# The token mixer of a hybrid decoder layer: chunk by chunk over all heads after the in-projection, or head pair by head pair between its last tiles

## What is computed

```python
x = x + 0.5 * post1(ffn1(pre1(x)))
P = pre_m(x) @ w_in        # 2816 columns: q 512 | k 128 | v 128 | hq 512 | hf 512 | hi 512 | hg 512
A = sliding-window attention(q, k, v)     # 8 query heads, 2 key heads, window 128, rotary, sinks
# HGRN2, 8 heads of 64: f = lb + (1-lb)*sigmoid(hf); k = 1-f; G = cumsum(log f)
#   S_new = exp(G_end) * S + (k*exp(G_end-G))^T hi ;  o = (hq*exp(G)) @ S + intra-chunk part
H = rms_norm(o) * silu(hg)
x = x + post_m(concat(A, H) @ w_out)
x = x + 0.5 * post2(ffn2(pre2(x)))
```

## Time and profile before

| what | value |
|---|---|
| median of three runs | 2332.66 us (2326.21 to 2344.02) |
| span of the profiled execution | 2344.2 us |
| its own time beside the span | not given apart; the highest of the three runs is 2344.02 us |
| in-projection, steady part 832 to 1062 us | TensorE busy 229.02 of 230, granted clock 1.00 |
| mixer, 1062 to 1390 us | TensorE busy 267.73 of 328, granted clock 0.73 |
| VectorE busy in the same 328 us | 230.07 |
| sample stage, 1390 to 1432 us | TensorE clock 0.54 |

### The profile page before, as it was taken

The page is one execution under the profiler, slowest core; times in us unless marked ns, Lnnn a source line. Parts: engine busy times, 40 slices in busy tenths (PEclk is TensorE's granted clock), DMA queues, the critical chain, the costliest instruction groups (busy, mean ns, idle before and its releaser), DMA issues.

```text
span 2344.2 us, 34327 instructions
## 1 busy us (share of the span) xinstructions
PE 2203.1 (94%) x13257; PEld 2071.8 (88%) x13257; DVE 1158.7 (49%) x1871; ACT 581.9 (25%) x852; POOL 428.6 (18%) x256
## 2 busy tenths in 40 slices
PE   6999999999999899997787887979999999999996
PEld 5999999999999799995555557969999999999996
DVE  3445444444544732226777665264444454444446
ACT  5111111111111631013343324162111111111113
POOL 6110010111110231103343311041111011110100
PEclk9999999999999999996777667989999999999998
DMA  3111111111111111110000001201111111111111
GB/s 120 55 46 45 54 45 40 49 45 45 45 54 46 75 63 54 45 45 19 0 0 0 31 31 52 108 18 55 46 45 54 36 45 54 45 45 54 45 36 72
DMA packets 28174, 108.83 MB, mean 46 GB/s; under 512 B 4178, under 2 KB 4826, under 8 KB 26337
## 3 DMA queue, kind: packets, MB, share of 16 engines
q1 hardware_dynamic: 28128, 108.20, 13.6%
HBM read 97.37 MB, written 10.81 MB: 46 GB/s over the span
## 4 chain that ended last, share of the span: by engine, by line
PE 84%; DVE 8%; ACT 3%; issue 3%; POOL 1%; DMA 0%; DVEq 0%; SPq 0%; ACTq 0%; POOLq 0%
PE PS L329 26%; PE PS L330 25%; PE PS L331 25%; DVE resid L1102 2%; PE PS L497 2%; PE PS L499 2%; PE PS L468 1%; PE PS L515 1%; DVE y L1097 1%; PE PS L365 1%; DVE dif L1296 1%; DVE q_dec L1307 1%; DVE mx L1358 1%; ACT sm L952 1%; DVE sm L1353 0%
## 5 line engine op out<-in xcount | busy, mean ns | idle before, releaser
L329 PE MATMUL PS<-x_hi,w_hi 128*128 128x344 f32 x2832 | 913.4, 323 | 49.5 <-DVE w_lo L1084 24.1
L330 PE MATMUL PS<-x_lo,w_hi 128*128 128x344 f32 x2832 | 908.1, 321 | 0.0
L331 PE MATMUL PS<-x_hi,w_lo 128*128 128x344 f32 x2832 | 906.7, 320 | 0.0
L329 PEld LDWEIGHTS PS<-x_hi,w_hi 128*128 128x128 f32 x2832 | 536.1, 189 | 54.3 <-issue 22.7
L330 PEld LDWEIGHTS PS<-x_lo,w_hi 128*128 128x128 f32 x2832 | 536.2, 189 | 0.9
L331 PEld LDWEIGHTS PS<-x_hi,w_lo 128*128 128x128 f32 x2832 | 536.1, 189 | 0.0
L624 POOL TENSOR_TENSOR raw<-raw,vecs 128x1024 f32<-128x1024 f32 x110 | 212.2, 1931 | 1439.1 <-DMA raw<-in_w_gu 1243.5
L1192 DVE TENSOR_TENSOR y<-y,PS 128x344 f32<-128x344 f32 x528 | 264.8, 511 | 182.9 <-PE PS L331 182.7
L329 PE MATMUL PS<-h,w_hi 128*128 128x344 f32 x1056 | 339.6, 322 | 0.7 <-DVE h L1156 0.3
L330 PE MATMUL PS<-h,w_hi 128*128 128x344 f32 x1056 | 337.6, 320 | 0.0
L331 PE MATMUL PS<-h,w_lo 128*128 128x344 f32 x1056 | 336.6, 319 | 0.0
(11 more groups left out here) (188 smaller groups left out, 1613.5 us busy)
## 6 DMA issues: line engine op xcount, KB each, us to landing
raw<-in_w_gu SPq DMA_DIRECT2D x88, 512.0 KB, 3.3
raw<-in_w_down SPq DMA_DIRECT2D x44, 512.0 KB, 3.3
raw<-in_w_in SPq DMA_DIRECT2D x22, 512.0 KB, 3.3
resid<-in_x SPq DMA_DIRECT2D x3, 1376.0 KB, 9.2
stream_x<-resid SPq DMA_DIRECT2D x3, 1376.0 KB, 4.7
resid<-stream_x SPq DMA_DIRECT2D x3, 1376.0 KB, 10.2
out_y<-resid SPq DMA_DIRECT2D x3, 1376.0 KB, 4.7
raw<-in_w_out SPq DMA_DIRECT2D x8, 512.0 KB, 3.3
```

The source lines that it names most:

```text
L329: nc.tensor.matmul(PS[:, bank, :GW], wh, vh, start=(k == 0), stop=False)
L330: nc.tensor.matmul(PS[:, bank, :GW], wh, vl, start=False, stop=False)
L331: mm = nc.tensor.matmul(PS[:, bank, :GW], wl, vh, start=False, stop=(k == last))
```

## The change

The in-projection's tiles get another order: k, v, q (4 tiles), then for each head pair hf, hq, hi, then hg. Nine tiles (`EARLY`) run as a stage of their own. Beside them keys and queries are rotated over all tokens (five times three matmuls of 344 columns, `rotate(r)`, and VectorE's `rope(r)`), and the values are transposed once for all chunks.

The other 13 tiles (39 units) are spread over eight bodies written out one after the other, five units a body, each cut into two halves of 12 matmuls that stand in the `gap`s of TensorE's order. Body i does one head pair (i // 2) for four chunks of HGRN, and all attention heads for chunk i. Gates are made per head pair: `gates(t+1)` on VectorE and `logs(t+1)` on ScalarE in the odd bodies, `sigmoid(t+1)` at the end of the even ones. The state becomes block diagonal (`Sbd`, 128 x 128 for a head pair), so that the part of the output that comes from the state is four full products; the four chunks' states are made one from the other on VectorE (`states()`), before TensorE may compute `outputs()`. The masked copies of a level become one instruction where they were two. The silu of hg moves behind the mixer. The samples' three loads are issued when the last body's attention has been copied, since their memory is in use till then. In the diff the orders of `body(i)` stand one after another: TensorE's (from `level(0)`), ScalarE's (from the second `level(1)`), VectorE's (from `def states()` with `seq`).

```diff
+T_K, T_V, T_Q, T_F, T_G = 0, 1, 2, 6, 18
+EARLY = 9
+BODIES, BODY_UNITS = 8, 5
...
-            sp.wait_ge(S["scan_done"], 4 * N_CH)
+            sp.wait_ge(S["attc_done"], N_CH)
+            sp.wait_ge(S["a_done"], 5 * BODIES)
             sp.dma_start(state_s[:], ins["state"]).then_inc(S["smp_in"], 16)
             sp.dma_start(k_win_s[:, :, 0:WINDOW - 1], ins["k_cache"]).then_inc(S["smp_in"], 16)
             sp.dma_start(v_win_s[0:WINDOW - 1], ins["v_cache"]).then_inc(S["smp_in"], 16)
...
+                def gap(x):
+                    if x // 2 < len(units) and units[x // 2] is not None:
+                        half_unit(units[x // 2], x % 2)
...
+                def outputs():
+                    pe.wait_ge(S["st_done"], i + 1)
+                    pe.wait_ge(S["k_done"], 7 * i + 2)
+                    pe.wait_ge(S["a_done"], 5 * i + 5)
+                    for j in range(TPH):
+                        nc.tensor.matmul(PS[:, 7, j * CH:(j + 1) * CH], Sbd[:, j, :], qg[:, j, :], start=(j == 0), stop=False,
+                                         skip_group_check=True)
+                    for hd in range(N_HEADS):
+                        j, r = hd // 2, slice(HEAD * (hd % 2), HEAD * (hd % 2 + 1))
+                        mm = nc.tensor.matmul(PS[r, 7, j * CH:(j + 1) * CH], V[:, TPH * b + j, r], A[:, hd, :],
+                                              start=False, stop=(hd >= N_HEADS - 2), skip_group_check=True)
+                    mm.then_inc(S["o_done"], 1)
...
                 level(0)
+                gap(0)
+                if b == 0:
+                    values()
+                gap(1)
                 level(1)
                 scores(0)
+                gap(2)
                 level(2)
+                gap(3)
                 level(3)
+                gap(4)
                 scores(1)
                 level(4)
+                gap(5)
+                keys_by_token()
+                gap(6)
                 probs_by_key(0)
+                gap(7)
+                states()
+                attend(0)
+                gap(8)
                 probs_by_key(1)
+                outputs()
+                gap(9)
+                attend(1)
...
                 level(1)
+                unit_end(0)
                 level(2)
+                if b == 1 and t < TPH - 1:
+                    logs(t + 1)
+                unit_end(1)
                 level(3)
                 level(4)
                 exponentials(0)
+                unit_end(2)
...
                 probs(0)
+                unit_end(3)
+                if i < BODIES - 1:
+                    first_decays(i + 1)
...
+                if b == 0 and t < TPH - 1:
+                    sigmoid(t + 1)
+                unit_end(4)
...
+                def states():
+                    if i:
+                        dve.wait_ge(S["o_done"], i)
...
+                    for j in range(TPH):
+                        for o in range(2):
+                            r = slice(HEAD * o, HEAD * (o + 1))
+                            dst = state[r, t, :] if b and j == TPH - 1 else Sbd[r, j + 1, r]
+                            up = nc.vector.scalar_tensor_tensor(dst, Sbd[r, j, r], g_end[r, j:j + 1], PS[r, 2, j * HEAD:(j + 1) * HEAD],
+                                                                ALU.mult, ALU.add)
+                        if j < TPH - 1:
+                            seq(up)
...
+                level(i, 2)
+                q_decayed(i, 1)
+                weights(0)
+                q_decayed(i, 2)
+                unit_end(0)
+                if b and t < TPH - 1:
+                    gates(t + 1)
+                level(i, 3)
+                weights(1)
+                q_decayed(i, 3)
                 sub_max(0)
+                unit_end(1)
+                level(i, 4)
                 weights(2)
+                q_decayed(i, 4)
                 weights(3)
                 over(0)
                 sub_max(1)
+                unit_end(2)
                 weights(4)
+                if i + 1 < BODIES:
+                    start(i + 1)
+                unit_end(3)
                 over(1)
+                if i + 1 < BODIES:
+                    q_decayed(i + 1, 0)
+                states()
+                unit_end(4)
```

More of the change, by code:

```diff
@@ L64, in __call__, with tile_of, body_units @@
         ins.then_inc(self.sem, 1)
[L65 to L73, removed]
+        self.eng.wait_ge(self.sem, self.n)
+def tile_of(v):
+    n = EARLY + v // NG
+    return n, v % NG, v % 2, n % 2
+def body_units(i):
+    first = BODY_UNITS * i
+    if i < BODIES - 1:
+        return [first + j for j in range(BODY_UNITS)]
+    return [None] + [v for v in range(first, N_LATE)]
 def build(nc, ins, outs):
@@ L747, in _ @@
+                normed(0)
+                for n in tiles[1:]:
+                    in_gain(n)
+                normed(1)
+                if i < BODIES - 1:
+                    first_keys(i + 1)
+            first_keys(0)
+            for i in range(BODIES):
+                body(i)
             for g in range(NG):
                 pool.wait_ge(S["cat_hi_a"], g + 1)
-                nc.gpsimd.tensor_tensor(x_lo[:, g, 0:TPH], q_reg[:, :, g * GW:(g + 1) * GW],
+                nc.gpsimd.tensor_tensor(x_lo[:, g, 0:TPH], Q[:, :, g * GW:(g + 1) * GW],
@@ new lines, in _, with body, unit_end @@
+            sigmoid(0)
+            in_split(EARLY)
+            logs(0)
+            first_decays(0)
+            in_split(EARLY + 1)
+            def body(i):
+                t, b, c, na = i // 2, i % 2, i, 2 if i else 1
+                ends = {v - BODY_UNITS * i: v // NG + EARLY + 2 for v in body_units(i) if v is not None and v % NG == NG - 1}
+                if i == BODIES - 1:
+                    ends = {x + 1: n for x, n in ends.items()}
+                def unit_end(x):
+                    if x in ends:
+                        in_split(ends[x])
@@ L1324, in start @@
                                         ALU.subtract).then_inc(S["d_done"], 1)
-                level(c, 1)
-            def body(c, more):
-                tok = bass.ds(c * CH, CH)
+                level(i, 1)
+            for n in range(2, EARLY):
+                in_split(n + 1)
+                if n == 2:
+                    dve.wait_ge(S["spilled"], 16 * NG)
+                    dve.wait_ge(S["mem_zero"], 3)
+                for g in range(NG):
+                    evac(n, g, g, 3 * n + g)
+                    if g == 0 and n <= 6:
+                        rope(n - 2)
+                    elif g == 0 and n == 7:
+                        gates(0)
+                    elif g == 0 and n == 8:
+                        start(0)
@@ L1344, in weights @@
[L1344 to L1356 removed]
+                    w, at_ = LEVELS[l - 1], M_LVL + (l - 1) * CH
```

900 lines of the change are left out of this document (448 added, 452 removed).

## The result

The kernel after takes 2343.76 us, median of 16 runs, and the kernel before 2331.44 in 16 runs beside it: ratio 1.005, 95% interval 1.0034 to 1.0066. That is half a per cent slower, inside the 1% that the forecast had set as no change, and 73 us less had been forecast. The profiled execution of after spans 2341.7 us and took 2343.85.

What follows compares the result with a forecast made beforehand. TensorE bounds the in-projection, a chain of handovers the mixer. Of a 468.6 us stretch, 10.6, 358 for bodies and 1.8 remain, gaining 98.2; the loads return 25, so 73 off 2332.7 gives 2259 us, range 2195 to 2318.

Steps and rivals of the forecast that it cites:

- What bounds the kernel, TensorE's and VectorE's work: TensorE bounds the in-projection, handovers the mixer; a new body has 37.5 us of TensorE work and 32 of VectorE.
- Walking one body: Following the waits from TensorE's `level(0)` gave bodies of 37 to 47 us, 341 us for all eight.
- Half the clock: In five bodies an idle time halves TensorE's clock for 4 to 8 us afterwards: 10 us added.
- GpSimd's gains: VectorE waits for GpSimd in thirteen gains in the bodies, half a us each: 7 us added, of 0 to 25 possible.
- What moves elsewhere: Rotations in the early tiles cost 8.6 us, values by token and the first body's wait for gates 2: 10.6 us.
- The samples' loads: Issued only after the last attention copy, they leave VectorE waiting 25 us in the open before the sample stage.
- The sum against the median: The gain of 73 us, worked out on the 2344.2 us profiled span, was taken off the 2332.7 median: 2259 us.
- the chain grows: Rival: ScalarE's and VectorE's waits for units lengthen the chain, bodies average 52 us, 416 in all, 2317 us; chance 0.22.
- TensorE bound: Rival: the waits overlap and the bodies take TensorE's floor, 292 us and some 10 for handovers, 2203 us; chance 0.17.
- slower: the clock: Rival: the bodies run mostly at 1.2 GHz; the gain is gone at mean clock 0.68, 2388 us at 0.60; chance 0.09.
- the signs given: In the bodies: TensorE near 90% busy, clock above 0.9, lengths 39 to 47 us, named waits; value cache waiting some 25 us.
- the case: The forecast's own main outcome for the whole kernel, 2225 to 2300 us; chance 0.50.

Runs made afterwards that it cites:

- e10: e8 with the samples' loads issued once the buffers under them are free, no longer all behind the last attention copy: 2250.48 us, ratio to the kernel before 0.9661.
- e5: Changed kernel with late weight splits, late value copies and the value cache loaded in two parts: 2293.65 us, ratio to the kernel before 0.9812.
- e4: Changed kernel with ScalarE's `hi_s` and `V` copies moved behind the exponentials of levels 1 and 2 in a pair's first body: 2326.48 us.
- e1: Changed kernel with the weight splits of tiles that end at unit 0 or 1 moved behind unit 2: 2321.79 us, 22.0 under the changed kernel.
- e9: Changed kernel with e4, e3 and twelve of thirteen weight splits placed where their unit has long ended: 2276.50 us, ratio to the kernel before 0.9765.
- e6: Changed kernel with copies in place of the sigmoid and logarithm of three head pairs, their results left out: 2332.32 us in one execution.
- e8: e9 with the next pair's sigmoid, gates and logarithm moved to other places in the bodies: 2257.14 us, ratio to the kernel before 0.9684.
- e3: Changed kernel with the samples' value cache loaded as 112 and 15 partitions in place of 127: 2326.05 us, 17.7 under the changed kernel.
- e11: Kernel before with the value cache loaded as 112 and 15 partitions: 2341.34 us beside 2332.68 for the kernel before, ratio 1.0022.
- e2: Changed kernel with 6 of 24 matmuls in each of the 39 units in the bodies: 2305.46 us, 38.3 under the changed kernel.
- e7: Changed kernel with GpSimd's 11 late gains applied to 8 of 1024 columns, the rest left out: 2334.26 us in one execution.

## Why the prediction was wrong

By its own steps:

- *What bounds the kernel, TensorE's and VectorE's work.* Right. VectorE's row was 32.3 us a body (32). By groups: `q_dec` of 64 x 256 took 691 ns and of 64 x 512 1371 on average in the bodies (the earlier trace rows had 470 and 1769), and the state steps 280 ns each, eight of them 2.2 us (2.0). TensorE's work with little waiting was 313 us in e10 (292 at full clock).
- **The step that failed is "Walking one body".** It gave 341 us for the bodies, with clock and GpSimd 358; they took 420. Of the 62 us, three parts can be named by the runs. They overlap, as e5 shows, so they aren't an exact sum.
  - The values' copy is not in the walk. The kernel puts `hi_s` and `V` ahead of level 1's exponential on ScalarE (the excerpt in the section on the change starts behind them), and the walk went from `level(0)` to `level(1)` with "no wait". It was worth 17.3 us (e4).
  - The splits are in the walk, for five bodies with 4 to 6 us each, some 25 us. They were worth 22.0 (e1) and 17.2 more (e9 against e5), some 39. Missed were, by the order on ScalarE, those at x = 2, which stand ahead of the decay for the states, those at x = 4, which stand ahead of the next body's level 1, and that VectorE's `w_lo` waits for ScalarE's `w_hi` (10.9 us, 7 times) with everything of VectorE behind it.
  - Sigmoid, logarithm and gates were put at 2 to 5 us in three bodies, 6 to 15. Replaced by copies they gave 11.4 (e6), and where they no longer wait for each other 15 to 19 (e8). The load was counted; the wait for VectorE's gates, 4.94 us in the row above, was not.
  - Beyond what the walk had for them these are 17, 14 and 5 to 9 us, up to 40 of the 62. The rest is in the plain body, which the walk put at 39 us. Without its splits and gates the walk comes to some 306 us, 323 with clock and GpSimd; e10, where these stand out of the way, needs 346.5. These 23 us no experiment took apart. VectorE's evacuations in a fixed order, as in body 2 of e1, are the likely place, and are argued and not shown.
- *Half the clock*: 10 us were added, for an idle time in each of five bodies; after's bodies hold 18 of over 2 us, and TensorE paid 38 us more than in e10, which itself has 313 for 292. That the clock halves behind such an idle time held in most places, body 2 among them, but not in all: behind 2.61 us at 1247.86 in after, and 3.10 at 1098.85 in e10, the units went on at full speed (0.32 us a matmul, against 0.49 elsewhere).
- *GpSimd's gains*: 7 us, half a us each for thirteen. Measured 9.5 for the 11 that there are, 0.86 each, in a single execution.
- *What moves elsewhere*: 10.6 us for the early tiles. From the `x1` store to the first `level(0)` 141.8 us passed, where 129.0 had been reckoned: 12.8. Near.
- *The samples' loads*: 25 us in the open; the stretch behind the last copy grew by 27.3. Right, with the cause: the value cache in two parts gave back 17.7 (e3), and e11 has nothing to gain.
- *The sum against the median.* The 73 us were worked out against the profiled execution, at the upper end of before's runs, and taken off the median, 14 us lower (2346 for its own time, if as much lies around the span as in after, against 2332.7). The forecast said that hardly anything lay between them; it took the highest of three runs for the profiled one's like and didn't weigh that the median was 11 us below. Of the 85 us by which 2259 was missed, 14 are this, 62 the bodies, 9 the three small items (2.2, 2.3, 4.2).

The rival that came true is "the chain grows", given 0.22: bodies of 52 us, 416 in all, against 52.5 and 420, with the mechanism that it names. Its time of 2317 was still low, by the same 14 us and the small items. "TensorE bound" is refuted by e2, "slower: the clock" by a clock of 0.86 in the bodies, though the clock took 38 us. Of the signs given, the bodies were neither 39 to 47 us nor at 90% and a clock above 0.9 (83% and 0.86), as the case would have had them; the waits for `q_dec` and for the value cache came as described.

That the repaired kernel e10 has bodies of 43.3 us, near the forecast's 44.75, doesn't make the walk right: the forecast had splits and gates in them, and e10 hasn't. The nearness is luck.

The Trainium skill (ScalarE: Activation LUTs, Table sets: the hidden batching unit) says a logarithm and an exponential can share one set and need one load. In the trace of after 1.28 us are paid on both sides of each logarithm in the bodies (1099.82 and 1107.13 above), as the forecast assumed against the page; the trace disagrees with the page.

## What to carry to other kernels

Walk the change on each engine's own order, line by line, and not only on the bounding one's: an instruction that waits for the bounding engine costs what stands behind it, however short it is itself. Work for a later tile goes to the first place in every queue where its condition has long been met, not to where it first becomes possible; here moving 12 splits, 8 small copies, 3 sigmoids, 3 gates and 3 logarithms, with no work removed, was worth some 69 us of 2344 (86.6 in e8, less the 17.7 of the value cache). Such waits hide one another: with one gone the next can show, as in body 2 of e1. When a stage is shortened or reordered, list the transfers that it covered; their length without cover is in the trace already.

## What the runs showed of the hardware

- While a transfer over 127 partitions (508 KB) was under way, 27 GB/s came in, and VectorE's wait ended 25 us after its issue; with 112 and 15 partitions VectorE waited 17.3 us less. The Trainium skill (DMA: Bandwidth & Descriptors, Why a DMA increments its semaphore by 16 and not by 1) says that 127 partitions put everything on one engine. By its rule, the largest divisor up to 16, 112 would use 16 engines; e3 agrees.
- A DMA issue can block behind such a transfer: SyncE's issue of `pick` took 10.96 us in after and 10.77 in e1, and 0.27 us in e3 and e5.
- TensorE stood 2.56 us, ran 512 columns in 1.13 us and then 1024 in 3.78; in e4 with no such idle time the two took 1.05 and 1.99. The same idle time doesn't always do the same: behind 1.95 us ahead of the first body, level 0 took 3.56 us in after and 1.97 in e1, e3, e4, e5, e9 and e10.
- Four elements took VectorE 0.17 us with GpSimd idle and 1.83 beside a GpSimd product of 1024 columns, ending within 0.02 us of it; taking most of 11 such products away was worth 9.5 us in the one execution of e7.
- Between two kernels with the same matmuls in the bodies, the granted clock was 0.86 and 0.95 and TensorE's busy time 351 and 313 us: half of what the waits cost didn't show as idle time.
